# Gated DeltaNet phase of a one-core decoder step: row scalings on GpSimd or on ScalarE and VectorE, and where q and k are turned

## What is computed

```
gc = cumsum(g, -1)
decay = exp(where(tri_incl, gc[..., :, None] - gc[..., None, :], -inf))
k_beta = k * beta[..., None]
A = where(tri_strict, einsum('bnhid,bnhjd->bnhij', k_beta, k) * decay, 0.0)
rhs = concatenate([v * beta[..., None], k_beta * exp(gc)[..., None]], -1)
sol = triangular_solve(eye(C) + A, rhs)          # u, w
qk = einsum('bnhid,bnhjd->bnhij', q, k) * decay
# scan over the chunks:
v_new = u_i - w_i @ S
o     = (q_i * exp(gc_i)) @ S + qk_i @ v_new
S     = S * exp(g_last) + (k_i * exp(g_last - gc_i)).T @ v_new
# afterwards
o = o * rsqrt(mean(o * o) + eps) * norm_g * silu(z)
```

## Time and profile before

| | us |
|---|---|
| median of 3 runs | 2177.58 |
| lowest and highest | 2176.33, 2180.63 |
| profiled execution, its own time | 2177.58 |
| its span | 2175.8 |
| `phase_delta`, from the barrier before it to the one behind it | 280.2 to 441.4 |

### The profile page before, as it was taken

The page is one execution under the profiler, slowest core; times in us unless marked ns, Lnnn a source line. Parts: engine busy times, 40 slices in busy tenths (PEclk is TensorE's granted clock), DMA queues, the critical chain, the costliest instruction groups (busy, mean ns, idle before and its releaser), DMA issues. The chain is left out here.

```text
span 2175.8 us, 33950 instructions
## 1 busy us (share of the span) xinstructions
PE 2088.1 (96%) x12934; PEld 1888.1 (87%) x12934; DVE 1633.2 (75%) x3056; ACT 789.4 (36%) x1297; POOL 548.5 (25%) x334
## 2 busy tenths in 40 slices
PE   8999989989999899999999999999989999999998
PEld 8998879878756699999999999999977777787776
DVE  6636667664252523999999889999968899898898
ACT  4335453332240222322334344444433333333332
POOL 0000020000000000031121035555537556665630
PEclk9999989999999899999999999999999999999999
DMA  5223210151432311486676668888899999999993
GB/s 166 80 97 113 83 46 1 54 184 40 174 136 99 97 60 30 155 317 227 236 268 208 210 224 333 334 333 333 333 362 385 386 382 385 384 388 381 387 369 115
DMA packets 223217, 483.76 MB, mean 222 GB/s; under 512 B 12015, under 2 KB 137199, under 8 KB 221446
## 3 DMA queue, kind: packets, MB, share of 16 engines
q1 hardware_dynamic: 177030, 314.56, 40.8%
q0 software_dynamic: 46080, 167.79, 21.1%
HBM read 423.29 MB, written 58.36 MB: 221 GB/s over the span
## 5 line engine op out<-in xcount | busy, mean ns | idle before, releaser
L2915 PE MATMUL ps<-v_high_low,gated_high_low 128*128 128x512 f32 x2304 | 533.9, 392 | 25.3 <-ACT gated_high_low L2983 20.9
L2915 PEld LDWEIGHTS ps<-v_high_low,gated_high_low 128*128 128x128 f32 x2304 | 432.8, 189 | 126.1 <-ACT v_high_low L2981 23.5
L2519 PE MATMUL ps<-x_high_low,u_high_low 128*128 128x384 f32 x1024 | 355.6, 347 | 0.2 <-ACT u_high_low L2585 0.2
L2520 PE MATMUL ps<-x_high_low,u_high_low 128*128 128x384 f32 x1024 | 345.0, 337 | 0.0
L3007 POOL DMA_INDIRECT outputs<-peer_v,kept x138 | 256.8, 1861 | 169.6 <-DVE kept L3024 136.5
L2636 POOL DMA_INDIRECT scores<-peer_u,kept x64 | 95.0, 1485 | 781.2 <-DVE kept L2756 604.3
L2594 ACT ACTIVATE kept<-ps 128x384 f32<-128x384 f32 x128 | 62.9, 491 | 407.0 <-PE ps L2524 403.8
L2524 PE MATMUL ps<-x_high_low,u_high_low 128*128 128x384 f32 x1024 | 204.7, 341 | 0.0
L2519 PEld LDWEIGHTS ps<-x_high_low,u_high_low 128*128 128x128 f32 x1024 | 192.5, 188 | 0.5 <-ACT u_high_low L2585 0.5
L2520 PEld LDWEIGHTS ps<-x_high_low,u_high_low 128*128 128x128 f32 x1024 | 192.8, 188 | 0.0
L3087 DVE TENSOR_TENSOR v_high_low<-raw_v,v_high_low 128x1024 fp32r<-128x1024 f32 x120 | 146.3, 1220 | 52.1 <-ACT v_high_low L2981 52.1
(11 more groups left out here) (455 smaller groups left out, 4244.8 us busy)
## 6 DMA issues: line engine op xcount, KB each, us to landing
experts<-peer_u SPq DMA_DIRECT2D x63, 1024.0 KB
raw_v<-peer_v SPq DMA_DIRECT2D x60, 1024.0 KB, 13.3
hidden<-kept SPq DMA_DIRECT2D x64, 384.0 KB
gates<-scores SPq DMA_DIRECT2D x12, 2048.0 KB
first_hidden<-hidden SPq DMA_DIRECT2D x16, 768.0 KB, 18.3
outputs<-gates SPq DMA_DIRECT2D x16, 768.0 KB
outputs<-hidden SPq DMA_DIRECT2D x16, 768.0 KB
first_gates<-gates SPq DMA_DIRECT2D x15, 768.0 KB
```

What stands on the lines that cost most here:

```text
L2519: pe.matmul(o, utr[:, b, HI, k], xr[:, HI, k, 0:DN], start=(k == 0), stop=False)
L2520: pe.matmul(o, utr[:, b, HI, k], xr[:, LO, k, 0:DN], start=False, stop=False)
L2915: ins = pe.matmul(bank(c, 2 * t + h), gr[:, slot, x, DN * b + P * t:DN * b + P * t + P], vr[:, slot, y, D * b + 512 * h:D * b + 512 * h + ...
```

## The change

Five edits in `phase_delta`:

1. The scalings of `decayed_keys`, `beta_values` and `gate_gains` leave ACT and DVE and are done by POOL, each as one 512-wide instruction for each block of rows (`rows` in the new POOL list). POOL scales the two decayed blocks of a tile once `prepared` and `turned3` allow it, then does L1470 and L1472 of that tile; behind the loop come the five blocks of beta values and the five of gate gains.
2. The 16 transposes of a tile stand together behind `prepared`; `turn_qk` is gone.
3. ACT copies the three turned blocks behind the exponentials of its own tile, instead of running the next tile's exponentials ahead.
4. Before the inverse DVE waits for the decayed keys of all five tiles, not four.
5. In the scan `norm_tile(n)` stands at the end of turn n, behind `mask_k(n + 1)`, instead of behind L1443 of turn n+1.

```diff
--- before.py
+++ after.py
@@ -1031,9 +1031,7 @@
     rms, rms_s, cleared = s("delta_rms"), s("sample_rms"), s("state_cleared")
     c.states_stored, c.wo_in0, c.wo_hi0 = c.shared_sem("delta_states_stored"), c.shared_sem("w_o_first_in"), c.shared_sem("w_o_first_high_set")
     w_o0, c.w_oh0 = words(c, M_G, 2, D), rounded(c, "w_o_high0", M_WOH, 2, D)
-    gain_set, bv_set, kg_set, unit_set, turned_qk = (s("delta_" + x) for x in (
-        "gate_gains_set", "beta_v_set", "decayed_k_set", "unit_rows_set", "q_and_k_turned"))
-    GAINS_AT = 8
+    gain_set, bv_set, kg_set = (s("delta_" + x) for x in ("gate_gains_set", "beta_v_set", "decayed_k_set"))
     items = [(lev, n) for lev in range(1, LEVELS) for n in range(NT) if n < 4 or lev < 2]
     item_no = {x: i for i, x in enumerate(items)}
 
@@ -1075,25 +1073,17 @@
                     ins = pe.matmul(bank(c, 1)[:, r * h:r * h + r], gb[0:r, h], ut, start=True, stop=True)
                 ins.then_inc(cums, 1)
 
-            def turn(n, sources):
-                r = ROWS[n]
-                for o, src in sources:
-                    for h in range(DNH):
-                        ins = pe.transpose(bank(c, o)[:, r * h:r * h + r], src[0:r, P * h:P * h + P], ident[0:r, 0:r])
-                return ins
-
-            def turn_qk(n):
-                pe.wait_ge(unit_set, n + 1)
-                turn(n, ((2, ct[:, n, 0:512]), (3, ct[:, n, 512:1024]))).then_inc(turned_qk, 1)
-
             cumulate(0)
-            turn_qk(0)
             for n in range(NT):
                 r = ROWS[n]
                 pe.wait_ge(prepared, n + 1)
                 if n:
+                    pe.wait_ge(turned3_act, n)
                     pe.wait_ge(turned3_dve, n)
-                turn(n, ((4, beta_k(n)), (5, qe))).then_inc(turned3, 1)
+                for i, src in enumerate((ct[:, n, 0:512], ct[:, n, 512:1024], beta_k(n), qe)):
+                    for h in range(DNH):
+                        ins = pe.transpose(bank(c, 2 + i)[:, r * h:r * h + r], src[0:r, P * h:P * h + P], ident[0:r, 0:r])
+                ins.then_inc(turned3, 1)
                 if n + 1 < NT:
                     cumulate(n + 1)
                 pe.wait_ge(turned3_act, n + 1)
@@ -1105,8 +1095,6 @@
                 for h in range(DNH):
                     ins = pe.matmul(bank(c, 7, 512, r)[:, r * h:r * h + r], q3[1][:, h], q3[0][:, h], start=True, stop=True)
                 ins.then_inc(kk, 1)
-                if n + 1 < NT:
-                    turn_qk(n + 1)
 
             pe.wait_ge(at_set, NT)
             for n in range(NT):
@@ -1215,7 +1203,8 @@
                     act.wait_ge(cums, n)
                 act.copy(gb[0:r], over(g[0:r, n], 2, [r, 4, P])).then_inc(spread, 1)
 
-            def row_exps(n):
+            spread_decay(0)
+            for n in range(NT):
                 r = ROWS[n]
                 act.wait_ge(gc_out, n + 1)
                 act.activation(eg[0:r, n], eg[0:r, n], ACT.Exp)
@@ -1226,41 +1215,12 @@
                 act.activation(dd, dd, ACT.Exp).then_inc(dd_exp, 1)
                 if n + 1 < NT:
                     spread_decay(n + 1)
-
-            def keep_turned(n):
-                r = ROWS[n]
-                act.wait_ge(turned_qk, n + 1)
+                act.wait_ge(turned3, n + 1)
                 if n >= 2:
                     act.wait_ge(kk, n - 1)
-                for i in range(2):
-                    act.copy(qkt[:, n % 2, i, 0:4 * r], bank(c, 2 + i, 4 * r))
-                act.wait_ge(turned3, n + 1)
-                act.copy(qkt[:, n % 2, 2, 0:4 * r], bank(c, 4, 4 * r)).then_inc(turned3_act, 1)
-
-            def decayed_keys(n):
-                r = ROWS[n]
-                act.wait_ge(exps, n + 1)
-                for h in range(DNH):
-                    act.activation(ct[0:r, n, P * h:P * h + P], beta_k(n)[0:r, P * h:P * h + P], ACT.Identity, scale=eg[0:r, n, h:h + 1])
-                for h in range(DNH):
-                    x = ct[0:r, n, 512 + P * h:640 + P * h]
-                    ins = act.activation(x, x, ACT.Identity, scale=eg[0:r, n, 4 + h:5 + h])
-                ins.then_inc(kg_set, 1)
-
-            def beta_values(n):
-                r = ROWS[n]
-                for h in range(DNH):
-                    x = ct[0:r, n, 1024 + P * h:1152 + P * h]
-                    ins = act.activation(x, x, ACT.Identity, scale=beta[0:r, n, h:h + 1])
-                return ins
-
-            spread_decay(0)
-            row_exps(0)
-            for n in range(NT):
-                keep_turned(n)
-                if n + 1 < NT:
-                    row_exps(n + 1)
-                    decayed_keys(n)
+                for i in range(3):
+                    ins = act.copy(qkt[:, n % 2, i, 0:4 * r], bank(c, 2 + i, 4 * r))
+                ins.then_inc(turned3_act, 1)
             for n in range(NT):
                 r = ROWS[n]
                 act.wait_ge(t0_turned, n + 1)
@@ -1269,12 +1229,6 @@
                 r = ROWS[n]
                 act.wait_ge(m1, i + 1)
                 act.copy(unit(A_M1, n, r), bank(c, i % 2, 4 * r, r).rearrange("p (h t) -> p h t", h=4)).then_inc(m1_out, 1)
-                if i == NT:
-                    decayed_keys(NT - 1)
-                elif i < NT - 1:
-                    beta_values(i)
-                elif i == NT - 1:
-                    beta_values(i).then_inc(bv_set, 1)
             for i, n in enumerate((4, 0, 1, 2, 3)):
                 r = ROWS[n]
                 act.wait_ge(uw, i + 1)
@@ -1333,7 +1287,6 @@
                 ins.then_inc(dd_set, 1)
 
             def prepare(n):
-                v.wait_ge(unit_set, n + 1)
                 v.wait_ge(exps, n + 1)
                 if n >= 2:
                     v.wait_ge(kg_set, n - 1)
@@ -1342,10 +1295,10 @@
 
             v.memset(eps[:], RMS_EPS)
             v.memset(ms[:], 1.0)
-            unit_length(0).then_inc(unit_set, 1)
+            step(unit_length(0))
             differences(0)
             prepare(0)
-            unit_length(1).then_inc(unit_set, 1)
+            step(unit_length(1))
             for n in range(NT):
                 r = ROWS[n]
                 if n + 1 < NT:
@@ -1357,7 +1310,7 @@
                 if n + 1 < NT:
                     prepare(n + 1)
                 if n + 2 < NT:
-                    unit_length(n + 2).then_inc(unit_set, 1)
+                    step(unit_length(n + 2))
                 v.wait_ge(dd_exp, n + 1)
                 dd = decays(n)
                 if n == 4:
@@ -1367,7 +1320,7 @@
                 v.tensor_tensor(unit(A_QK, n, r), bank(c, 7, 4 * r, r).rearrange("p (h t) -> p h t", h=4), dd, ALU.mult).then_inc(at_set, 1)
 
             v.wait_ge(at_set, NT)
-            v.wait_ge(kg_set, NT - 1)
+            v.wait_ge(kg_set, NT)
 
             def mask_a(i):
                 lev, n = items[i]
@@ -1384,13 +1337,6 @@
                 for a, b_ in ((A_T, 2), (A_TT, 4))[is_last(lev, n):]:
                     ins = v.tensor_tensor(unit(a, n, r), unit(a, n, r), bank(c, b_ + i % 2, 4 * r, r).rearrange("p (h t) -> p h t", h=4), ALU.subtract)
                 ins.then_inc(t_new, 1)
-
-            def gate_gains(n):
-                r = ROWS[n]
-                z = hd[0:r, n, 8:520].rearrange("p (h k) -> p h k", h=4)
-                if n == 0:
-                    v.wait_ge(gain_in, 16)
-                v.tensor_tensor(z, z, over(ng[0:r], 1, [r, 4, P]), ALU.mult).then_inc(gain_set, 1)
 
             mask_a(0)
             mask_a(1)
@@ -1398,8 +1344,6 @@
                 if i + 2 < len(items):
                     mask_a(i + 2)
                 update(i)
-                if GAINS_AT <= i < GAINS_AT + NT:
-                    gate_gains(i - GAINS_AT)
             v.memset(s_p[:], 0.0).then_inc(cleared, 1)
             v.wait_ge(states_in, 16)
             bm = cst(c, K_BM, NB * SAMP).rearrange("p (b t) -> p b t", b=NB)
@@ -1421,7 +1365,7 @@
                     mask_w(0)
                     mask_k(0)
             v.wait_ge(u_out, NT)
-            v.wait_ge(gain_set, NT)
+            v.wait_ge(gain_set, 1)
 
             def norm(o, z, scale, rows_, heads):
                 step(v.reciprocal(scale, scale))
@@ -1442,7 +1386,6 @@
                 v.wait_ge(ws_s, n + 1)
                 v.tensor_tensor(vs[:, n], ct[0:SAMP, 4, 1024 + P * n:1152 + P * n], bank(c, 0, 512, SAMP)[:, P * n:P * n + P], ALU.subtract).then_inc(vnew_s, 1)
                 if n:
-                    norm_tile(n - 1)
                     norm_head(n - 1)
                 v.wait_ge(od, n + 1)
                 for h in range(DNH):
@@ -1458,18 +1401,39 @@
                 ins.then_inc(s_new_s, 1)
                 if n < 3:
                     mask_k(n + 1)
+                    norm_tile(n)
             norm_tile(3)
             step(norm_head(3))
 
         @block.gpsimd
         def _(pool):
+            def rows(n, a, scale, k, src=None):
+
+                r = ROWS[n]
+                o = ct[0:r, n, a:a + 512].rearrange("p (h k) -> p h k", h=4)
```

(16 more changed lines are left out.)

## The result

The changed kernel takes 2199.94 us (median of 4 runs, 2197.85 to 2202.18) against 2178.39 of the kernel before: ratio 1.0102, 95% interval 1.009 to 1.0114. It is slower by about 21.5 us; forecast were 2196.6 and a range of 2185 to 2205.

The account below looks back on a forecast made before the run. DVE was taken to set the preparation's pitch, PE to bound the inverse, DVE to be just behind PE in the scan. Preparation 14.4, inverse 0 and scan 4.6 gave +19.0 on 2177.6: 2196.6 us, range 2185 to 2205.

Parts of the forecast that it names:

- The scan edit: Scan: `norm_tile` before L1441 is covered by nothing, so 1.53 us is paid after three turns, +4.6 us.
- The bound with a falling clock: Scan: if PE's longer pause halves its clock, up to 1.7 us more in each of three turns, 9.7 us.
- Rival 2: Preparation: POOL hardly blocks DVE, only L1324 for long; pitch 6.8 us, +7.0 in all, 2184.6 us; chance 0.12.
- The 14.4: Preparation in all: 4.0 for the first tile, 9.7 for three pitches and 0.7 at the end, +14.4 us.
- The first tile: Preparation: PE idles beforehand and turns this tile cold, copies at 296.5 against 292.54, +4.0 us (warm +1.9).
- The three pitches: Preparation: time from tile to tile 9.7 us, the middle of 8.8 and 10.6, against 6.47; +9.7 us.
- the next zero is 6.2 + 0.6 + 1.3 + 0.6 + 0.1: Preparation, full clock: DVE's two copies and POOL's decayed-key instructions exclude each other, so a tile's pitch is 8.8 us.
- rival 3: POOL's scaling with a repeated operand is slow, up to 2.5 us each; +10 on the forecast, 2206 us; chance 0.08.
- rival 1: PE's clock stays up in the preparation: +14.2 us in all, 2191.8 us; chance 0.17.
- The end: Preparation's end: the fifth tile's first inverse level waits for its decayed keys on POOL, +0.7 us, between 0 and 2.6.
- L1377 may stand up to 1.27 for each in about 5 items ... I take 0: Inverse: POOL's ten instructions delay DVE's masks beyond 0.8 us of slack, at most +2.5 us, taken as 0.
- What was removed: ACT's 60 short instructions save nothing (bound 0 to 0.7 us); gate gains leaving DVE save at most 1.7, taken as 0.

Follow-up runs that it names:

- b_keys: The kernel before with the decayed keys alone on POOL, two instructions for each tile: 2183.07 us, ratio 1.0016.
- b_turns: The kernel before with all 16 transposes of a tile behind the scaled copies, the scalings left on ACT and DVE: 2184.32 us, ratio 1.0029.
- b_scan: The kernel before with the scan edit alone (`norm_tile(n)` at the end of turn n): 2183.32 us, ratio 1.0021.
- b_best: The kernel before with the decays read from PSUM and `mask_k(n)` of the scan behind L1443 instead of before L1441: 2175.53 us, ratio 0.9986.
- b_psum: The kernel before, where L1324 and L1325 read the sums of the decays from PSUM instead of their SBUF copy: 2176.26 us, ratio 0.9990.
- u_pause: The changed kernel, where POOL waits for each of its ten beta and gain instructions before it issues the next: 2190.2 us, ratio 1.0049.
- b_train: The kernel before with only the beta values and gate gains moved to POOL, ten instructions in a row behind its loop: 2183.2 us, ratio 1.0021.
- u_paced: The changed kernel with POOL's ten instructions spread over the inverse, each waiting for the first product of a later item: 2193.71 us, ratio 1.0069.
- u_gains: The changed kernel with the gate gains back on DVE, so that POOL's row is five instructions: 2196.43 us, ratio 1.0084.
- u_pairs: The changed kernel with a wait of POOL on its own semaphore after every second of its ten instructions: 2189.91 us, ratio 1.0049.

## Why the prediction held, and where it didn't

1. **The scan edit: right.** 4.6 forecast, 5.0 measured, of which 3 x 1.54 is the wait at L1190; alone it cost +4.6. The bound with a falling clock wasn't needed: the granted clock was 0.95 in this scan, and 0.94 in those of b_keys and b_turns, which have the order of before and take 46.4 us.
2. **DVE and POOL exclude each other: right.** The copies stood, those with a PSUM input didn't, and reading PSUM took the stall off L1324. The Trainium skill, "SBUF — State Buffer", section "SBUF: two separate sides", agrees in this, and the 1.49 us of POOL beside DVE's copy shows that it holds in both directions. Where it speaks of a wait for one whole instruction, the masks that stood for several of POOL's go beyond it, and there the measurement decides (point 4). Rival 2 is out.
3. **The size of the preparation: too large.** The 14.4 hold 0.7 for the stage to L1145, so 13.7 stand against +7.8 measured. The first tile: +4.0 forecast, +3.5 measured (298.03 - 282.21 against 292.54 - 280.24). It is turned at the low clock, as forecast, but b_scan and b_best, where the code of this tile is that of before, are 1.9 and 2.1 us longer there too; so part of the 3.5 may be chance. The three pitches: +9.7 forecast, +5.0 measured. Two steps failed. One is "the next zero is 6.2 + 0.6 + 1.3 + 0.6 + 0.1", which has DVE's copies stand 0.7 + 1.3 = 2.0 us in every tile: they stood 0.5 + 0.8 in the first of the three pitches (1.17 and 1.52 instead of 0.68), 0.8 in the last, and not at all in the middle one. POOL's new instructions took 1.03 us there, not 1.27 (the 2.5 of rival 3 is out too). The other is the clock, taken as low for half of each tile: the granted clock was 0.81 in the middle pitch (9.1 us) and 1.00 in the other two (8.1 and 7.2 us), so rival 1 is nearer here. The end was 0.65 us shorter, not longer: PE turned the fifth tile in 1.17 us instead of 1.91, as its granted clock was 0.84 from there to L1118, and 0.50 before. By the ends of DVE's copies this last part takes 3.4 us here, and between 3.2 and 4.0 us in before, b_scan, b_psum and b_best, so that difference says nothing of the change.
4. **The ten instructions in the inverse: wrong.** "L1377 may stand up to 1.27 for each in about 5 items ... I take 0" failed. I priced each mask against one POOL instruction, where the first mask that came too late stood for eight of the row: +9.0 in that stage, against the 0.7 of the sum and an upper bound of +2.5 for the masks. The pause run, in which the same work costs nothing that can be told from noise there (6.4 us; the kernels without the row have 5.6 to 6.6), shows that it is the row without a gap. The later wait for the fifth decayed keys, which I placed "under L1118", has a part in it: it held the first mask from 325.7 to 328.2, so that the second was due at 329.1, just before the row. In b_train, without that wait, two masks were through and only the third was caught, for 6.1 us. No run has the changed kernel without this wait alone, so its share of the 9.0 is argued and not shown.
5. **What was removed: right.** ACT's loss of 60 instructions and the gate gains brought nothing that can be seen; the inverse itself is as long as before. One sentence was wrong without harm: that `exps` comes later on ACT. The order of copies and exponentials on ACT is the same in both kernels, so the third edit changes only that the first two copies of a tile wait for all 16 transposes.
6. **Not forecast:** u and w took 1.6 us more. The granted clock of PE was 0.58 from 406.0 to 409.5, that is mostly the lower of its two levels, right after the small instructions of the 32-row tile:

```profile
406.00:409.50 3.50, 3.50 (x21) 3.50 (x20) 2.80 (x5) 0.59 (x1) 0.00 (x0) 0.58 0.00 0
```

Four of the kernels in the table have it (the changed one, b_keys, u_paced, u_gains) and the others don't, among them u_pause with the same instructions there. So the change does not bring it by itself; what does isn't shown.

So the total was near by luck in half of it: 5.9 us too much in the preparation, and 8.3 (the row), 1.6 (u and w) and 0.4 (the scan) too little behind it, leave 4.4 between the forecast and the phase of the profile. Right were the kind of the stall in the preparation and the scan; the largest single term, the row, was missing. The four parts alone add 0.21 + 0.21 + 0.16 + 0.29 = 0.87%, against 1.02% of all; the row costs more in the changed kernel, 9.0 against 6.1, where it catches an earlier mask. Each of these ratios has an interval of about 0.1% either way, so the sum and the whole can't be told apart with certainty.

What stays open is why a waiting DVE instruction passes POOL in some seams (between two of POOL's instructions without a gap) and not in others. Candidates such as the state of POOL's queue at the moment of the request were not tried by themselves.

## To carry to other kernels

Before work is given to POOL, list what DVE does with SBUF operands alone in that stretch, and price the wait at up to the length of POOL's row without a gap, not of one instruction (here up to eight of ten, and four of five); if the row must stand there, let POOL wait on its own semaphore after each or every second instruction. In these traces a DVE instruction on a critical chain was out of POOL's reach once an input came from PSUM (L1324, L1325, L1330), where these data were anyway. And where the next engine already waits 0.2 us for an instruction, what is put ahead of it is paid in full (1.53 us of `norm_tile`, 1.54 us more wait).

## What the runs showed of the hardware

- Beside rows of POOL instructions without a gap a ready DVE mask took 9.58, 6.42 and 4.93 us (changed kernel, b_train, u_gains: rows of ten, ten and five); with a gap after each 1.94 and after every second 2.93 us (u_pause, u_pairs). Its own 0.69 us is in all of them.
- POOL's two-input instruction on 128x512 fp32 took 1.03 us where one input is a scale repeated along the row, and 1.25 to 1.27 where both inputs vary along the row, with no DVE instruction in its way (changed kernel).
- Reading a PSUM source instead of SBUF made the 128x4 copy 0.16 us beside POOL (b_psum), instead of 0.84 to 0.85 (before).
